# Delta rule: the transposed inverse turned on TensorE, and one state product per chunk and head

## The reference

```python
L = jnp.where(strict, jnp.einsum('bnhcd,bnhed->bnhce', kb, k) * decay, 0.0)
a = L + jnp.eye(CHUNK)
rhs = jnp.concatenate([v * beta[..., None], kb * jnp.exp(gc)[..., None]], -1)
sol = lax.linalg.triangular_solve(a, rhs, left_side=True, lower=True, unit_diagonal=True)
u, w = sol[..., :Dv], sol[..., Dv:]
...
def step(state, inp):
    qd, kd, uu, ww, aqk, gl = inp
    v_new = uu - ww @ state                 # V
    o = qd @ state + aqk @ v_new
    state = state * gl + kd.T @ v_new
    return state, o
```

## Time and profile before

| | |
|---|---|
| time, median of 3 runs (lowest, highest) | 2439.64 us (2436.48, 2440.57) |
| the profiled execution | 2436.78 us, its span 2435.1 us |
| TensorE matmuls (PE) busy | 2378.7 us, 98%, 13689 instructions |
| TensorE weight loads (PEld) busy | 2078.4 us |
| VectorE (DVE), ScalarE (ACT), GpSimd (POOL) busy | 1477.3, 1065.9, 247.1 us |
| mean granted clock of TensorE | 0.995 |

### The profile page before, as it was taken

The page is one execution under the profiler, slowest core; times in us unless marked ns, Lnnn a source line. Parts: engine busy times, 40 slices in busy tenths (PEclk is TensorE's granted clock), DMA queues, the critical chain, the costliest instruction groups (busy, mean ns, idle before and its releaser), DMA issues.

```text
span 2435.1 us, 35464 instructions
## 1 busy us (share of the span) xinstructions
PE 2378.7 (98%) x13689; PEld 2078.4 (85%) x13689; DVE 1477.3 (61%) x1563; ACT 1065.9 (44%) x1332; POOL 247.1 (10%) x222
## 2 busy tenths in 40 slices
PE   8999989999999999999999999998999999999998
PEld 7888878888888888888999899977888888888887
DVE  6654567556546555567767758566764555555556
ACT  4455444434434444444635436343443443443442
POOL 0151001001001000000032311310100000000000
PEclk9999999999999999999999999999999999999999
DMA  6653456565665566555524425246465656656554
GB/s 236 187 160 113 148 181 199 197 191 181 200 191 189 192 185 195 195 202 148 165 79 131 122 79 165 70 139 198 139 199 193 189 191 196 186 192 194 182 199 156
DMA packets 236672, 417.09 MB, mean 171 GB/s; under 512 B 23761, under 2 KB 46570, under 8 KB 234986
## 3 DMA queue, kind: packets, MB, share of 16 engines
q1 hardware_dynamic: 235162, 410.73, 53.1%
q10 hardware_dynamic: 1360, 4.19, 0.4%
HBM read 412.77 MB, written 2.10 MB: 170 GB/s over the span
## 4 chain that ended last, share of the span: by engine, by line
PE 83%; issue 11%; DVE 3%; POOL 2%; ACT 1%; DMA 1%; SPq 0%; ACTq 0%; DVEq 0%; POOLq 0%
PE quad L600 20%; PE quad L629 11%; PE quad L627 11%; PE quad L628 11%; PE quad L603 10%; PE quad L571 4%; PE quad L573 4%; PE quad L575 4%; PE quad L1078 1%; PE quad L1065 1%; PE quad L1075 1%; ACT whi L1177 1%; PE quad L669 1%; DMA raw<-in_mem_w_kv 1%; PE quad L1111 0%
## 5 line engine op out<-in xcount | busy, mean ns | idle before, releaser
L1573 DVE TENSOR_TENSOR wlo<-raw,whi 128x1024 fp32r<-128x1024 f32 x760 | 981.6, 1299 | 713.6 <-ACT whi L1177 711.5
L1177 ACT ACTIVATE whi<-raw 128x1024 fp32r<-128x1024 f32 x760 | 799.8, 1058 | 987.5 <-PE quad L629 517.9
L600 PE MATMUL quad<-xs,whi 128*128 128x512 f32 x2048 | 649.6, 397 | 7.1 <-DVE xs L1890 3.7
L627 PE MATMUL quad<-whi,hh 128*128 128x512 f32 x1248 | 488.6, 392 | 2.2 <-POOL hl L2225 1.3
L629 PE MATMUL quad<-whi,hl 128*128 128x512 f32 x1248 | 485.8, 389 | 0.0
L628 PE MATMUL quad<-wlo,hh 128*128 128x512 f32 x1248 | 485.6, 389 | 0.0
L603 PEld LDWEIGHTS quad<-xs,wlo 128*128 128x128 f32 x2048 | 386.7, 189 | 91.0
L603 PE MATMUL quad<-xs,wlo 128*128 128x256 f32 x2048 | 404.1, 279 | 0.4 <-issue 0.4
L600 PEld LDWEIGHTS quad<-xs,whi 128*128 128x128 f32 x2048 | 314.5, 189 | 9.9 <-issue 4.9
L627 PEld LDWEIGHTS quad<-whi,hh 128*128 128x128 f32 x1248 | 234.3, 188 | 50.8 <-POOL hl L2225 1.7
L629 PEld LDWEIGHTS quad<-whi,hl 128*128 128x128 f32 x1248 | 234.2, 188 | 48.8
(11 more groups left out here) (311 smaller groups left out, 2309.9 us busy)
## 6 DMA issues: line engine op xcount, KB each, us to landing
raw<-in_mlp_w SPq DMA_DIRECT2D x512, 512.0 KB
raw<-in_gdn_w_in SPq DMA_DIRECT2D x105, 512.0 KB
raw<-in_w_out SPq DMA_DIRECT2D x64, 512.0 KB
raw<-in_mem_w_kv SPq DMA_DIRECT2D x32, 512.0 KB
raw<-in_mla_w_in SPq DMA_DIRECT2D x25, 512.0 KB
raw<-in_mla_w_ukv SPq DMA_DIRECT2D x24, 256.0 KB
gb<-in_ln_g SPq DMA_DIRECT2D x4, 1024.0 KB, 6.5
gb<-in_ln_b SPq DMA_DIRECT2D x4, 1024.0 KB, 8.5
```

The costliest lines, as they stand in the source:

```text
L600: last = nc.tensor.matmul(both, b.whi[:, slot, k, cols], b.xs[:, :, kt, :], start=start, stop=stop, skip_group_check=True)
L627: nc.tensor.matmul(ps[:, t, 0:n], ah[:, kt, toks], hi[:, k, 0:n], start=start, stop=False)
L1177: nc.scalar.activation(b.whi[:, c % NSPLIT], b.raw[:, slot], ACT.Copy).then_inc(sem.hi_ready, 1)
L1573: nc.vector.tensor_tensor(b.wlo[:, c % NSPLIT], b.raw[:, c % NRAW], b.whi[:, c % NSPLIT].bitcast(F32), ALU.subtract).then_inc(sem.lo_ready, 1)
```

## The change

1. Z^T is made only at level 5. At levels 2 to 5 the X of the level before is transposed on TensorE right behind the two Y blocks, and VectorE copies it to `xt`.
2. VectorE's list of a level becomes: copies to `xt` (from level 2), `feed(1)`, then the adds to `xi` (at level 5 the add to `xt`).
3. ScalarE's copies of Y no longer wait for Z^T.
4. ScalarE puts negated W and decayed Q of a chunk side by side into one buffer `wq`. From j = 1 one product with 128 stationary columns replaces the two of 64: half of the bank's rows is W's part, the other half the start of the output. The bank of chunk j is chosen by `chunk_bank`; before chunk 3 TensorE waits for the first output copy.
5. `kt` and `xi` lie where `zr` is; `wt` and `qdt` are gone.

```diff
+def out_half(j):
+    c = j % 2 if j == 0 else 1 - j % 2
+    return slice(CHUNK * c, CHUNK * (c + 1))
...
-    b.kt, o = at("kt", quad, F32, o)
...
-    b.qdt, o = at("qdt", quad, F32, o)
+    b.wq, o = at("wq", [P, TT, GH, 4, CHUNK], F32, o)
...
-    b.xi = b.wt = b.kt
+    b.kt = b.xi = b.zr
...
 # TensorE
+            def chunk_bank(j):
+                return (side_ps[0], turn_ps[0], side_ps[1], side_ps[0])[j]
...
+                    if l > 1:
+                        for t in tiles:
+                            each(lambda h, o, s_: nc.tensor.transpose(o, b.xi[:, t, h, :], b.ident[:, :]),
+                                 side_ps[t], sem.p_xt)
                     beside(g, 6 + l)
...
-                        each(lambda h, o, s_: nc.tensor.matmul(o, b.ys[:, t, h, :], b.xt[:, t, h, :], start=s_,
-                                                               stop=True, skip_group_check=True),
-                             side_ps[t], sem.p_zt)
+                        else:
+                            each(lambda h, o, s_: nc.tensor.matmul(o, b.ys[:, t, h, :], b.xt[:, t, h, :], start=s_,
+                                                                   stop=True, skip_group_check=True),
+                                 side_ps[t], sem.p_zt)
...
                         pe.wait_ge(sem.d_s, g * (NC - 1) + j)
-                        each(lambda h, o, s_: nc.tensor.matmul(o[r, :], b.wt[:, t, h, r], state[:, h, :], start=s_,
-                                                               stop=True, skip_group_check=True), turn_ps[0], sem.p_vn)
                         if j == 2:
                             pe.wait_ge(sem.d_u, n0 + 2)
-                        for h in range(GH):
-                            nc.tensor.matmul(side_ps[t][r, h * P:(h + 1) * P], b.qdt[:, t, h, r], state[:, h, :],
-                                             start=h == 0, stop=False, skip_group_check=True)
+                        if j == NC - 1:
+                            pe.wait_ge(sem.a_o, g * NC + 1)
+                        each(lambda h, o, s_: nc.tensor.matmul(o, b.wq[:, t, h, 2 * c:2 * c + 2, :].rearrange("p a i -> p (a i)"),
+                                                               state[:, h, :], start=s_, stop=False, skip_group_check=True),
+                             bank, sem.p_vn)
                         beside(g, 6 + LEVELS - 1 + j)
...
 # ScalarE
-                    bank_out(b.qdt, t, turn_ps, sem.a_qdt)
+                    nc.scalar.activation(b.wq[:, t, :, 1:3, :], turn_ps[t][:, :].rearrange("p (h c i) -> p h c i", h=GH, c=2),
+                                         ACT.Copy).then_inc(sem.a_qdt, 1)
...
-                        if l > 1:
-
-                            act.wait_ge(sem.p_zt, (g * (LEVELS - 1) + l - 2) * TT + t + 1)
...
-                    bank_out(b.wt, t, turn_ps, sem.a_w, scale=-1.0)
+                    nc.scalar.activation(b.wq[:, t, :, 0:4:3, :], turn_ps[t][:, :].rearrange("p (h c i) -> p h c i", h=GH, c=2),
+                                         ACT.Copy, scale=-1.0).then_inc(sem.a_w, 1)
...
 # VectorE
                 for l in range(1, LEVELS):
+                    if l > 1:
+                        for t in range(TT):
+                            dve.wait_ge(sem.p_xt, (g * (LEVELS - 2) + l - 2) * TT + t + 1)
+                            nc.vector.tensor_copy(b.xt[:, t].rearrange("p h c -> p (h c)"),
+                                                  side_ps[t][:, :]).then_inc(sem.d_xt, 1)
+                    feed(1)
                     for t in range(TT):
-                        m = (g * LEVELS + l) * TT + t
                         if l < LEVELS - 1:
                             dve.wait_ge(sem.p_z, (g * (LEVELS - 2) + l - 1) * TT + t + 1)
                             x_ = b.xi[:, t].rearrange("p h c -> p (h c)")
                             nc.vector.tensor_tensor(x_, turn_ps[t][:, :], x_, ALU.add).then_inc(sem.d_x, 1)
-                        dve.wait_ge(sem.p_zt, (g * (LEVELS - 1) + l - 1) * TT + t + 1)
-                        x_ = b.xt[:, t].rearrange("p h c -> p (h c)")
-                        nc.vector.tensor_tensor(x_, side_ps[t][:, :], x_, ALU.add).then_inc(sem.d_xt, 1)
-                    feed(1)
+                        else:
+                            dve.wait_ge(sem.p_zt, n0 + t + 1)
+                            x_ = b.xt[:, t].rearrange("p h c -> p (h c)")
+                            nc.vector.tensor_tensor(x_, side_ps[t][:, :], x_, ALU.add).then_inc(sem.d_xt, 1)
```

More of the change, by code:

```diff
@@ L360, in __init__ @@
         self.p_zt = signal("p_zt")
+        self.p_xt = signal("p_xt")
         self.p_w = signal("p_w")
@@ L1090, in gdn @@
                 for j in range(NC):
-                    t = j // 2
-                    r = slice(CHUNK * (j % 2), CHUNK * (j % 2 + 1))
+                    t, c = j // 2, j % 2
+                    r = slice(CHUNK * c, CHUNK * (c + 1))
+                    ro = out_half(j)
                     m = g * NC + j
                     state = b.st[:, j % 2]
+                    bank = chunk_bank(j)
                     if j:
                         pe.wait_ge(sem.d_s, g * (NC - 1) + j)
-                        each(lambda h, o, s_: nc.tensor.matmul(o[r, :], b.wt[:, t, h, r], state[:, h, :], start=s_,
-                                                               stop=True, skip_group_check=True), turn_ps[0], sem.p_vn)
                         if j == 2:
                             pe.wait_ge(sem.d_u, n0 + 2)
-                        for h in range(GH):
-                            nc.tensor.matmul(side_ps[t][r, h * P:(h + 1) * P], b.qdt[:, t, h, r], state[:, h, :],
-                                             start=h == 0, stop=False, skip_group_check=True)
+                        if j == NC - 1:
[3 more added lines that the diff above has]
+                             bank, sem.p_vn)
                         beside(g, 6 + LEVELS - 1 + j)
@@ L1110, in gdn @@
                         pe.wait_ge(sem.d_u, n0 + 1)
-                    each(lambda h, o, s_: nc.tensor.matmul(o[r, :], b.aq[r, t, h, r], b.vn[r, 0, h, :],
+                    each(lambda h, o, s_: nc.tensor.matmul(o[ro, :], b.aq[r, t, h, r], b.vn[r, 0, h, :],
                                                            start=j == 0 and s_, stop=True, skip_group_check=True),
-                         side_ps[t], sem.p_o)
+                         bank, sem.p_o)
                 beside(g, 6 + LEVELS - 1 + NC)
@@ L1519, in gdn @@
                     act.wait_ge(sem.p_o, g * NC + j + 1)
[L1520 removed]
+                    nc.scalar.activation(b.orow[r, j // 2].rearrange("p h c -> p (h c)"), chunk_bank(j)[out_half(j), :],
                                          ACT.Copy).then_inc(sem.a_o, 1)
@@ L2120, in gdn @@
                             dve.wait_ge(sem.d_u, n0 + t + 1)
-                        nc.vector.tensor_tensor(vn, turn_ps[0][r, :], uu, ALU.add).then_inc(sem.d_vn, 1)
+                        nc.vector.tensor_tensor(vn, chunk_bank(j)[r, :], uu, ALU.add).then_inc(sem.d_vn, 1)
                     if j == NC - 1:
```

## The result

The changed kernel takes 2448.3 us in the median of five runs (2446.33 to 2451.47), where the kernel before takes 2439.64 (2436.48 to 2440.57, five runs): ratio 1.0042, 95% interval 1.0029 to 1.0055 (the ratio is formed over all runs; the two medians alone give 1.0036). It is slower, by 8.7 us in the medians. A second comparison on one chip gave 2447.21 against 2439.76 us, ratio 1.0027 (1.0015 to 1.0039). The time is inside the range of 2437 to 2451 and the direction of the sum, +3.8, is right; but most of the chance stood on "no change", and that it was not.

A forecast was written before the change was run, and what follows sets the result against it. TensorE's own instruction stream was taken to bound the kernel. Terms -21.4 + 10.4 - 9.0 + 14.1 + 5.5 + 4.2 = +3.8 us took the median from 2439.64 to 2443.4 us, range 2437 to 2451.

The forecast's parts named there:

- The split holds up X: Inverse levels: VectorE's split ahead of the X adds waits for ScalarE's `whi`; TensorE waits +14.1, +5.5, +4.2 us; chance 0.74.
- What goes and comes on TensorE: TensorE's stream: Z^T blocks out -21.4 us, transposes in +10.4, state and query products merged -9.0.
- The sum in the stage: All terms for inverse and state chunks together: -21.4 + 10.4 - 9.0 + 14.1 + 5.5 + 4.2 = +3.8 us.
- the bound of 0.2%: Whole kernel: 4.9 us, about what a measurement can tell from no change; the forecast lay 1.1 us inside it.
- my terms: Whole kernel: restart costs and the merge's 8.3 to 9.8 us give +2.0 to +5.6 us, 2441.6 to 2445.2.
- the split wouldn't hold: Inverse levels: VectorE's chunk has its `whi` already, waits only 0.18 us in 12 places; -17.8 us, 2421.8; chance 0.12.
- ScalarE's gapped copies of W hold up the state: State chunks: second W copy, in gapped runs, delays the first state product, restarts at upper end; 2446; chance 0.10.
- The X^T copies: VectorE's copies of the transposes from PSUM, beside GpSimd's mask products: covered before the next Z, costing nothing.
- The clock as I put it: Inverse: some 15 idle spells with transposes near each halve TensorE's clock; 36 us, 2475 and more; chance 0.04.
- the wait of 2.23 us at 181 us: Earlier trace: a TensorE wait with transposes behind it in a stretch at clock 1.00, evidence against the clock rival's fall.

The follow-up runs named there:

- late split: Changed kernel with VectorE one split behind: its feed after the scaling of K taken out, one added behind level 5; 2430.5 us, ratio 0.9964 to the kernel before.
- split-last kernel: Changed kernel with VectorE's feed put back behind the adds of each level; 2428.59 us, again 2427.63 us, ratios 0.9957 and 0.9955 to the kernel before.

## Why the prediction was right, and what was mis-sized

**The split holds up X.** Right, step by step: `whi` at +0.26, `wlo` at +1.35, X at +2.49 against 2.48, Y at +3.32 and 0.07 slower than in a stream, so +3.39 in effect against 3.35. A middle level is 8.92 us long against 8.87. At level 1 3.59 and 0.07 against 3.63, W at +3.22 and 0.10 against 3.35. Waits of 21.1 us in 15 places against some 20. The late split shows that the wait for ScalarE's half is the cause, the split-last kernel what it costs: 20.1 us.

**What goes and comes on TensorE.** The merged product saves 8.9 us against 9.0, a transposed pair costs 0.875 us against 0.87. By the rule of the Trainium skill (TensorE: Matmul & The Clock Gate, Terms: transpose mode 4 times faster for FP32) doubling the transposes would have cost an estimated 5.4 us; the run has 10.5, and the measurement decides.

**The sum in the stage.** 4.4 us against 3.8. The difference is 0.05 us a middle level and roundings of the same size elsewhere.

**The step that was mis-sized** is the last one, from the stage to the whole kernel: "made against the profiled execution, 2436.78 becomes 2440.6", and the median by the same 3.8. It takes all that lies outside the stage as unchanged. The medians of the two comparisons have 4.3 and 3.1 us more than the stretch's 4.4; the lower mean clock of such kernels accounts for 2.5 of that on average, and the rest is not explained. The stage alone would have been 0.18%, inside the bound of 0.2%, where I gave 0.54; what came on top put the result beyond it, for which I gave 0.34 (the interval of the second comparison still reaches down to 0.15%). The median of 2448.3 lies above all that my terms allow (2441.6 to 2445.2). The range held it only because it had the spread of the runs added on both sides, and not because I had foreseen a cost there: that much is luck.

**The rivals.** That the split wouldn't hold (0.12) is out: `whi` starts 0.26 us after Z in the trace after, as the equal counts in the earlier trace rows had said. That ScalarE's gapped copies of W hold up the state is out: 0.60 us, as without gaps. The X^T copies take 1.29 us the pair with GpSimd's products beside them, so nothing holds them up either. The clock as I put it, falling at the new waits, is out too: it is 1.00 through 15 waits of 1.3 to 1.7 us, 12 of them with transposes behind. The Trainium skill (the same page, Part 4: PE-mode transpose) says that transposes do not count as busy in the same way as matmuls; whatever that does, with 0.87 us of them in a level of 8.92 it brought no fall here. My other evidence for a steady clock, the wait of 2.23 us at 181 us, was in part luck: the clock held there in eight of thirteen profiles.

**The better version.** With VectorE's feed behind the adds, all else as changed, the kernel takes 2427.6 to 2428.6 us, 0.43% to 0.45% less than before. It beats both.

## What to carry to other kernels

An engine that runs its list in order lends every wait in it to all that stands behind: before moving a piece of filler work ahead of a hand-over, ask what this piece itself waits for, and count the instructions in the trace to learn which item it is. Work removed between a hand-over and its reader was cover; the 21.4 us of blocks taken out here were worth nothing while the add was done 3.2 us after its operand's block began, and some 17 us once one line moved (about 4 us of waits and late restarts stay). Measure the stage of a change by a stretch between two of its own instructions: it repeated within 0.1 us where the whole time of the kernel before spread over 8 to 10.

## What the runs showed of the hardware that was not expected

TensorE's wait for issue at the head of the MLP loops differs between executions of one kernel: 2.9 us and 3.9 in two profiles of the changed one, 0.6 and 1.0 in two of the one before. The short falls of the clock come in some executions and not in others at the same wait of the same code (2.2 us near 182 us: 1.00 in eight profiles, 0.83 in five), and the mean clock was lower by 0.0013 in the kernels with the changed inverse, outside the stage where this runs.
